# Ring order and modulation chunks in the prologue of a fused two-layer kernel: half of the features first

## The chip, the cores and the metric

The kernel runs on 1 core of one Trainium2 chip. The metric is device microseconds of one execution, as the median of 3 runs. A profile of one execution comes with it.

## The reference, cut to what matters

The reference computes a first block of two layers (gated MLP branch, grouped attention, bidirectional mLSTM), then a second block with dilated attention, a forgetting mixer and expert layers. The change touches only the start of layer 0 of the first block. There, for the latent rows `x` (256 x 1024) and the context rows `ctx` (256 x 1024):

```python
mod_lat = silu(c) @ w_ada[l] + b_ada[l]            # 1024 x 3072: shift, scale, gate, 1024 each
sh, sc, gt = jnp.split(mod_lat, 3, axis=-1)
xn = rms_norm(x, g_norm) * (1 + sc) + sh           # the same for ctx with silu(c_ctx)
...
p = xn @ w_in                                      # 1024 x 3344, in 7 column chunks
```

All of it is in float32. A product of float32 accuracy is made from rounded parts: high x high, high x low, low x high, three matmuls.

## The kernel before

**Ring.** All large weights come through a ring of 6 slots of 1 MB each, in the order of `ring_items()` (L86). An item is half of a chunk (512 of the 1024 rows, 512 columns: 1 MB; the first `w_in` chunk has 272 columns: 0.54 MB). SyncE (SP) walks through the list in order: before it issues item n, it waits until item n-6 is used up (`free(n - RING)`, issue at L322). A first half of a `w_in` chunk is used up once TensorE has done the fourth of the chunk's eight feature blocks (`win_used`), a second half at the chunk's end, an `ada` item once its eight matmuls are done. Between ring items stand, on the same queue, six small loads before item 10 (`EARLY_BEFORE`) and 21 small loads before item 22 (`LATE_BEFORE`, L442): gains, biases, router weights, `w_s`.

The list before: `ada` chunks 0, 1, 2, 3 of layer 0 (items 0 to 7), `w_in` chunk 0 (8, 9), first half of `w_in` chunk 1 (10), `ada` 4 and 5 (11 to 14), second half of `w_in` 1 (15), first half of `w_in` 2 (16), `ada` 0 of layer 1 (17, 18), second half of `w_in` 2 (19), first half of `w_in` 3 (20), `ada` 1 and 2 of layer 1 (21 to 24), second half of `w_in` 3 (25), and so on to item 37.

**Modulation.** A modulation chunk is 512 columns of `w_ada`: `ada_rows` (L2856) multiplies them on TensorE into a PSUM bank (16 matmuls), VectorE copies the bank to SBUF (`ada_copy`, L2271), `ada_row_cols` (L2869) sums and transposes it by 8 small matmuls, VectorE adds the bias (`ada_sums`). Chunks 0 and 1 are the shift of features 0 to 511 and 512 to 1023, chunks 2 and 3 the scale. After all four, VectorE makes `A1 = (1 + scale) * g_norm` and signals `mods_done`.

**Rows.** ScalarE squares and scales the four row tiles (`first_rows`), TensorE transposes them in 8 feature blocks k into PSUM (`norm`, L2823), ScalarE (even k) and VectorE (odd k) apply scale and shift (`transposed_block`, L1995 and L2312), ScalarE rounds to the high part `XH` (L2003), VectorE makes the low part `XL` (L2195).

**Projection.** `project_split` (L2950 to L2952) runs a chunk: for each of the 8 blocks k, four row tiles, three matmuls each. GpSimd (POOL) splits the weights into `WH` (L1852) and `WL` (L1861); the low part of block q comes in its program after the high part of block q+1. Behind chunk k come `ada_row_cols` of what `MODS_BEHIND[0][k-2]` names and `ada_rows` of what `MODS_BEHIND[0][k]` names.

**Hankel.** Six small matmuls on a one-hot table (L3315) make bias rows for the second block. VectorE splits them (L2800), POOL writes them to DRAM and waits for that before it splits any weights.

Of the kernel before, what the change touches and what calls it, by code (L numbers as in the profile page):

```python
# [23 lines left out]
KB = D // 128  # L24
# [59 lines left out]
def ring_items():  # L84
# [52 lines left out]
def build(nc, A, out):  # L137

    es = ExitStack()
    with es:  # L140
# [72 lines left out]
        YP = split("YP", 2 * KB * 256, xt_at).rearrange("p (s k n) -> p s k n", s=2, k=KB)  # L213
        PH = split("PH", 12288, p_at)
        OH = split("OH", 2048, x_at)
        ps = es.enter_context(nc.psum_tensor("ps", [128, 4096], F32))[:, :]
# [47 lines left out]
        for name in ("const_in", "rows_in", "rows_late", "x_in", "oh_in", "chain_dve", "chain_act", "pe_freed", "dve_freed",  # L264
                     "vec_T", "vec_cols", "silu_e", "silu_done", "ada_sums", "ada_cols", "mods_done",
                     "sq_sum", "xs", "xs_T", "xt_act", "xt_dve", "proj", "evict", "a2d", "d2a", "p2d", "d2p",
                     "p2a", "a2p", "row_scores", "row_max", "row_sum", "row_log", "max_rows", "max_T", "shift_rows", "scores", "probs",
# [112 lines left out]

        ADA_ORDER = [(0, ch) for ch in range(4)] + [it[1:] for n in range(7) for it in MODS_BEHIND[0].get(n, ())]

# [4 lines left out]
        def ada_rows_at(a):  # L387

            return bank(3 + a % 3) if a < 4 else bank(4 + a % 3)

# [4 lines left out]
        def ada_cols_at(a):  # L395

            return bank(7 - a % 2 if a < 4 else 7, 8 * a, 8 * a + 8)

# [219 lines left out]
        def pool_block2(pool):  # L618

            def table(part, v, dst, sem_):  # L620
# [5 lines left out]
                pool.dma_start(dst[:, :, 0:cols], src.bitcast(F32R)).then_inc(sem_, 16)  # L626

            pool.wait_ge(S("x_tile"), X_BLOCK1)
            nc.gpsimd.tensor_copy(jrev, K[:, K_J:K_J + 128]).then_inc(S("rounded"), 1)
# [1198 lines left out]
        def _(pool):  # L1828
# [66 lines left out]
        def _(act):  # L1895
# [93 lines left out]

            def transposed_block(k, tiles, scale, shift, dst=None):  # L1990

                act.wait_ge(S("xs_T"), c.up("xs_T", 2) - 1)
                for s in ((0, 1) if len(tiles) == 4 else (0,)):
                    lo, hi = (256, 512) if s == 0 else (0, 256)
                    ins = s_.activation(XT[:, k, lo:hi] if dst is None else dst[:, k, :], bank(k, lo, hi), ACT.Identity,  # L1995
                                        scale=scale(s)[:, k:k + 1], bias=shift(s)[:, k:k + 1])
                ins.then_inc(S("xt_act"), 1)

            def first_layer_rows(scale, shift):

                def high(k):
                    act.wait_ge(S("xt_act" if k % 2 == 0 else "xt_dve"), k // 2 + 1)
                    s_.activation(XH[:, k], XT[:, k], ACT.Copy).then_inc(S("xt_hi"), 1)  # L2003

                first_rows()
                act.wait_ge(S("mods_done"), 1)
                transposed_block(0, range(T), scale, shift)
                transposed_block(2, range(T), scale, shift)
                act.wait_ge(S("hk_out"), 16)
                high(0)  # L2010
                high(1)
                for k in (2, 4, 6):
                    if k + 2 < KB:
                        transposed_block(k + 2, range(T), scale, shift)
                    high(k)
                    high(k + 1)

# [163 lines left out]
        def _(dve):  # L2181
# [99 lines left out]
            def mods(kind, l):  # L2281
# [14 lines left out]
                to("mods_done", ins)  # L2296

            def invert_rstd(tiles):
# [7 lines left out]

            def transposed_block(k, tiles, scale, shift, dst=None):

                dve.wait_ge(S("xs_T"), c.up("xs_T", 2))
                for s in ((0, 1) if len(tiles) == 4 else (0,)):  # L2310
                    lo, hi = (256, 512) if s == 0 else (0, 256)
                    ins = v.tensor_scalar(XT[:, k, lo:hi] if dst is None else dst[:, k, :], bank(k, lo, hi), scale(s)[:, k:k + 1],  # L2312
                                          shift(s)[:, k:k + 1], ALU.mult, ALU.add)
                ins.then_inc(S("xt_dve"), 1)

            def first_layer_rows(scale, shift):
# [9 lines left out]
                for k in (2, 4, 6):  # L2326
                    if k + 2 < KB:
                        transposed_block(k + 3, range(T), scale, shift)
                    low(k)
# [467 lines left out]
            for g in range(3):  # L2797
                dve.wait_ge(S("hk_ps"), g + 1)
                hi, lo = (Qf[0:48, (3 * a + g) * HANKEL:(3 * a + g + 1) * HANKEL] for a in range(2))
                link(v.tensor_copy(hi.bitcast(F32R), bank(g, 0, HANKEL)[0:48, :]))  # L2800
                ins = tt(lo.bitcast(F32R), bank(g, 0, HANKEL)[0:48, :], hi, ALU.subtract)
# [15 lines left out]
        def _(pe):  # L2817
# [54 lines left out]

            def norm(tiles, blocks=range(KB)):
                for k in blocks:
                    for t in tiles:
                        if k == 0:
                            pe.wait_ge(S("xs"), c.up("xs"))
                        ins = tp(bank(k, 128 * t, 128 * t + 128), XS[:, t, 128 * k:128 * k + 128])
                    ins.then_inc(S("xs_T"), 1)
                if k == KB - 1:  # L2880
                    c.up("xt_act", 4)
                    c.up("xt_dve", 4)
                    pe.wait_ge(S("xt_act"), 2)
                    pe.wait_ge(S("xt_dve"), 2)

# [50 lines left out]
            def project_split(n, behind):  # L2936
# [3 lines left out]
                for k in range(KB):  # L2940
# [245 lines left out]
            def block1(l):  # L3186
                L = list(range(T)) if l == 0 else list(LAT)
                n = len(L)
                pe.wait_ge(S("mods_done"), l + 1)
                if l == 0:  # L3190
                    norm(range(T), range(6, KB))
                else:
                    norm_by_tile(range(T), before_last=5, before_chunks=3)
# [115 lines left out]
            ada_rows(0, 0)  # L3309
            ada_rows(0, 1)  # L3310
            pe.wait_ge(S("oh_in"), 16)
            pe.wait_ge(S("rel_in"), 16)
            pe.wait_ge(S("chain_pool"), 1)
            for g in range(3):
                mm(bank(g, 0, HANKEL)[0:48, :], RELB[0:33, :], Pf[0:33, 5000 + g * HANKEL:5000 + (g + 1) * HANKEL],  # L3315
                   start=True, stop=True).then_inc(S("hk_ps"), 1)
# [79 lines left out]
```

## Time and profile before

| | |
|---|---|
| median of 3 runs | 1562.59 us (1561.2 to 1564.77) |
| the profiled execution's own time | 1561.28 us |
| its span | 1559.5 us |
| TensorE busy | 1462.7 us (94%) |
| VectorE, ScalarE, GpSimd busy | 1020.8, 698.0, 224.0 us |
| HBM read | 283.77 MB, mean 183 GB/s |

Times in the trace are microseconds from the span's start. PE is TensorE's matmuls, SPq, POOLq and the like are an engine's queue where it issues DMAs. In a timeline a row is: start, duration, engine, line, operation, output and input, shapes, count; in square brackets the idle time before it and what ended it. Matmuls overlap in their pipeline, so the step between two starts is their cost, not the shown duration.

### The profile page before, as it was taken

The page shows a single profiled execution, that of the slowest core. Times are in us where ns is not written, and L with a number is a line of the kernel's source. Part 1 is how long each engine was busy: PE and PEld are TensorE (multiplying, and loading weights), DVE is VectorE, ACT ScalarE, POOL GpSimd, SP SyncE. Part 2 cuts the span into 40 slices and gives each one's busy share as a digit, 9 for nine tenths or more (in the row PEclk, how much of TensorE's full clock was granted, in tenths as well). Part 3 has the DMA queues.
Part 4 walks back from the last instruction along what each step waited for, and adds up shares of the span by engine and source line. Part 5 has one row for each costly group of instructions (what it writes and reads, how often), then busy time and mean ns, then how long its engine had stood idle before and what let it go on. Part 6 is the DMA issues. An engine that isn't in the chain of part 4 may idle for free.

```text
span 1559.5 us, 19666 instructions
## 1 busy us (share of the span) xinstructions
PE 1462.7 (94%) x7579; PEld 1092.4 (70%) x7579; DVE 1020.8 (65%) x1595; ACT 698.0 (45%) x1129; POOL 224.0 (14%) x240
## 2 busy tenths in 40 slices
PE   5999997989999889999999999899999998889998
PEld 2777772577655454788788877778887876678886
DVE  2418757764475863777677768687775656478776
ACT  3311228323211633655156524556654656356654
POOL 1558721133000201000310020000000004000000
PEclk8999999989999899999999999899998998999999
DMA  9585621202575433677676662398884420098882
GB/s 343 187 264 194 225 68 63 75 28 82 185 247 187 143 116 119 190 245 244 158 226 234 225 183 68 118 324 295 297 275 166 162 93 1 1 314 304 294 302 108
DMA packets 186474, 286.55 MB, mean 184 GB/s; under 512 B 13739, under 2 KB 95115, under 8 KB 186380
## 3 DMA queue, kind: packets, MB, share of 16 engines
q1 hardware_dynamic: 172080, 273.56, 51.4%
q0 software_dynamic: 13200, 8.84, 3.0%
q10 hardware_dynamic: 1100, 2.89, 0.5%
q8 instruction: 60, 0.98, 0.3%
q14 instruction: 34, 0.28, 0.1%
HBM read 283.77 MB, written 1.49 MB: 183 GB/s over the span
## 4 chain that ended last, share of the span: by engine, by line
PE 77%; DVE 13%; ACT 5%; DMA 2%; issue 1%; SPq 1%; POOL 0%; DVEq 0%; ACTq 0%; POOLq 0%
PE ps L1330 40%; PE ps L2932 6%; PE ps L2823 3%; PE ps L2950 3%; PE ps L2952 2%; PE ps L2951 2%; DVE acc L2240 2%; DMA ring<-in_w_ada 2%; ACT ps L2079 2%; DVE P L2195 2%; PE ps L3021 1%; SPq L442 1%; PE ps L2856 1%; PE ps L3004 1%; PE ps L1564 1%
## 5 line engine op out<-in xcount | busy, mean ns | idle before, releaser
L1330 PE MATMUL ps<-WB,YP 128*128 128x512 f32 x1196 | 290.7, 398 | 2.7 <-DVE WB L2195 2.7
L1330 PEld LDWEIGHTS ps<-WB,YP 128*128 128x128 f32 x1196 | 228.7, 193 | 51.5 <-issue 2.2
L2195 DVE TENSOR_TENSOR WP<-ring,WP 128x2048 fp32r<-128x2048 f32 (+1 forms) x102 | 219.2, 2164 | 49.0 <-ACT WP L818 48.8
L1330 PE MATMUL ps<-WP,XP 128*128 128x512 f32 x960 | 231.5, 393 | 6.3 <-DVE WP L2195 6.3
L1330 PEld LDWEIGHTS ps<-WP,XP 128*128 128x128 f32 x960 | 177.6, 188 | 44.5 <-DVE XP L2195 5.0
L818 ACT ACTIVATE WP<-ring 128x2048 fp32r<-128x2048 f32 x94 | 179.5, 1914 | 38.4 <-PE ps L1330 38.4
L2195 DVE TENSOR_TENSOR WB<-ring,WB 128x512 fp32r<-128x512 f32 x192 | 128.1, 690 | 87.5 <-ACT WB L672 85.7
L672 ACT ACTIVATE WB<-ring 128x512 fp32r<-128x512 f32 x192 | 114.1, 628 | 55.0 <-PE ps L1330 55.0
L2932 PE MATMUL ps<-ring,XT 128*128 128x512 f32 (+3 forms) x384 | 132.3, 501 | 1.1 <-ACT XT L2022 1.1
L2240 DVE SCALAR_TENSOR_TENSOR acc<-ring,silu_c,acc 128x512 f32<-128x512 f32 x168 | 127.0, 756 | 4.4
L1330 PE MATMUL ps<-WP,HP 128*128 128x512 f32 x480 | 114.7, 391 | 0.0
L2022 ACT ACTIVATE P<-ps 128x512 f32<-128x512 f32 (+3 forms) x66 | 35.2, 545 | 166.7 <-PE ps L2952 87.5
L2932 PEld LDWEIGHTS ps<-ring,XT 128*128 128x128 f32 x384 | 70.3, 192 | 56.4 <-issue 50.4
L1330 PEld LDWEIGHTS ps<-WP,HP 128*128 128x128 f32 x480 | 90.1, 188 | 19.6 <-issue 1.0
L2950 PE MATMUL ps<-WH,XH 128*128 128x512 f32 (+1 forms) x224 | 86.0, 384 | 2.2 <-DVE XL L2195 1.9
L2951 PE MATMUL ps<-WL,XH 128*128 128x512 f32 (+1 forms) x224 | 84.7, 378 | 0.0
L2952 PE MATMUL ps<-WH,XL 128*128 128x512 f32 (+1 forms) x224 | 84.7, 378 | 0.0
L2453 DVE TENSOR_REDUCE small<-ps 128x2 f32<-128x256 f32 (+3 forms) x68 | 53.5, 786 | 43.8 <-PE ps L1595 18.5
L1861 POOL TENSOR_TENSOR WL<-ring,WH 128x512 fp32r<-128x512 f32 (+1 forms) x56 | 79.9, 1428 | 0.1
L626 POOL DMA_DIRECT2D HBH<-hankel x24 | 16.9, 707 | 283.9 <-PE ps L1631 256.5
L739 ACT ACTIVATE E<-ps 128x512 f32<-128x512 f32 (+1 forms) x24 | 16.1, 670 | 85.6 <-PE ps L1631 43.9
L2950 PEld LDWEIGHTS ps<-WH,XH 128*128 128x128 f32 x224 | 42.8, 191 | 14.4 <-issue 4.2
(420 smaller groups left out, 2279.5 us busy)
## 6 DMA issues: line engine op xcount, KB each, us to landing
ring<-in_w_ada SPq DMA_DIRECT2D x72, 1024.0 KB, 7.5
ring<-in_a_w_in SPq DMA_DIRECT2D x36, 1024.0 KB, 5.2
ring<-in_w_gate SPq DMA_DIRECT2D x64, 512.0 KB, 4.4
ring<-in_w_up SPq DMA_DIRECT2D x64, 512.0 KB, 5.4
ring<-in_w_down SPq DMA_DIRECT2D x32, 1024.0 KB, 6.6
ring<-in_w_in SPq DMA_DIRECT2D x24, 1024.0 KB, 9.6
ring<-in_b_w_in SPq DMA_DIRECT2D x12, 1024.0 KB, 5.0
ring<-in_w_out SPq DMA_DIRECT2D x8, 1024.0 KB, 5.1
```

Source lines behind the costliest of these rows:

```text
L672: s_.activation(block_slot(q)[:, 0], w, ACT.Copy).then_inc(S("b_hi"), 1)
L818: s_.activation(WP[:, (m + 1) % CONV, 0], slot(first + m), ACT.Copy).then_inc(S("w_hi"), 1)
L1330: ins = mm(dst, x(a), w(b), start=(start and n == 0), stop=(stop_ and n == 2))
L1861: nc.gpsimd.tensor_tensor(lo, w, hi.bitcast(F32), ALU.subtract).then_inc(S("win_lo"), 1)
L2195: return v.tensor_tensor(out_, a, b, op)
L2240: ins = v.scalar_tensor_tensor(o, w[:, kk, :], sc, o, ALU.mult, ALU.add)
L2453: ins = v.tensor_reduce(o[n], src, AX.X, ALU.max, negate=True)
L2823: return nc.tensor.transpose(o, i, ident[0:n, 0:n])
L2932: ins = mm(b[:, 0:hi - lo], lhs(half * kk + k, t), w[:, k, lo:hi], start=(half == 0 and k == 0), stop=(half == len(its) - 1 and k == kk - 1))
L2950: mm(b, XH[:, k, cols], hi, start=(k == 0), stop=False)
L2951: mm(b, XH[:, k, cols], lo, start=False, stop=False)
L2952: ins = mm(b, XL[:, k, cols], hi, start=False, stop=(k == KB - 1))
```

## The change

It does six things.

1. The first ten ring items become `ada` 0, `ada` 2, first half of `w_in` 0, `ada` 1, `ada` 3, second half of `w_in` 0.
2. `MODS_BEHIND[0]` goes from two, one, two, one, two chunks behind `w_in` chunks 0 to 4 to one, two, one, two, two. By the rule of the list this gives: 10 `w_in` 1 first half; 11, 12 `ada` 4; 13 `w_in` 1 second half; 14 `w_in` 2 first half; 15, 16 `ada` 5; 17, 18 `ada` 0 of layer 1; 19 `w_in` 2 second half; 20 `w_in` 3 first half; 21, 22 `ada` 1 of layer 1; 23 `w_in` 3 second half; 24 `w_in` 4 first half; 25 to 28 `ada` 2 and 3 of layer 1; 29, 30 second half of `w_in` 4 and first half of 5; 31 to 34 `ada` 4 and 5 of layer 1. From item 31 on both lists are the same. `EARLY_BEFORE` and `LATE_BEFORE` stay 10 and 22.
3. TensorE starts with `ada` 0, the hankel matmuls, `ada` 2 and their columns, transposes feature blocks 0 to 3 and starts `w_in` chunk 0. `ada` 1, `ada` 3, their columns and the transposes of blocks 4 to 7 are put between its blocks 0 to 3.
4. VectorE makes `A1` by halves (`first_mods`, signals `mods_half` and `mods_done`), and scales row tile 2 itself; ScalarE scales the other three.
5. The hankel parts are kept in `P` rather than `Q`; POOL waits for their store only at the start of the second block. ScalarE's sqrt table is loaded before the squares.
6. PSUM homes of the rows, columns and transposed blocks are other banks; `ada_rows` waits from its eighth chunk on until the copy of the chunk three before it is made.

```diff
-MODS_BEHIND = ({0: (('ada', 0, 4), ('ada', 0, 5)), 1: (('ada', 1, 0),), 2: (('ada', 1, 1), ('ada', 1, 2)), 3: (('ada', 1, 3),), 4: (('ada', 1, 4), ('ada', 1, 5))},
+MODS_BEHIND = ({0: (('ada', 0, 4),), 1: (('ada', 0, 5), ('ada', 1, 0)), 2: (('ada', 1, 1),), 3: (('ada', 1, 2), ('ada', 1, 3)), 4: (('ada', 1, 4), ('ada', 1, 5))},
...
+FIRST_MODS = (0, 2, 1, 3)
...
-    for c in range(4):
-        chunk("ada", 0, c * 512, c * 512 + 512)
-    chunk("win", 0, *CHUNKS[0])
+    for half in range(2):
+        for c in FIRST_MODS[2 * half:2 * half + 2]:
+            chunk("ada", 0, c * 512, c * 512 + 512)
+        items.append(("win", 0, *CHUNKS[0], half))
...
@@ GpSimd @@
-                           Qf[0:48, 0:6 * HANKEL].rearrange("c (g j) -> c g j", g=6)).then_inc(S("hk_out"), 16)
-            pool.wait_ge(S("hk_out"), 16)
+                           Pf[0:48, 7000:7000 + 6 * HANKEL].rearrange("c (g j) -> c g j", g=6)).then_inc(S("hk_out"), 16)
...
@@ ScalarE @@
             def first_rows():
 
+                roots_ready()
...
-                for t in range(T):
+                for t in (0, 1, 3):
                     s_.activation(XS[:, t, :], X[:, t, :], ACT.Identity, scale=rstd[:, t:t + 1]
...
                 first_rows()
+                act.wait_ge(S("mods_half"), 1)
+                transposed_block(0, range(T), scale, shift, home=first_home)
+                high(0)
+                transposed_block(2, range(T), scale, shift, home=first_home)
+                high(1)
+                high(2)
+                high(3)
                 act.wait_ge(S("mods_done"), 1)
-                transposed_block(0, range(T), scale, shift)
-                transposed_block(2, range(T), scale, shift)
+                transposed_block(4, range(T), scale, shift, home=first_home)
+                high(4)
+                high(5)
+                transposed_block(6, range(T), scale, shift, home=first_home)
+                high(6)
+                high(7)
                 act.wait_ge(S("hk_out"), 16)
...
@@ VectorE @@
-                transposed_block(1, range(T), scale, shift)
-                transposed_block(3, range(T), scale, shift)
+                transposed_block(1, range(T), scale, shift, home=first_home)
                 low(0)
+                transposed_block(3, range(T), scale, shift, home=first_home)
                 low(1)
...
+                low(2)
+                ada_copy(0, 1)
+                low(3)
+                ada_sums(3, [(0, 1)])
+                ada_copy(0, 3)
+                ada_sums(4, [(0, 3)])
+                to("mods_done", first_mods(4))
...
             invert_rstd(range(T))
-            for ch in range(1, 4):
-                ada_copy(0, ch)
-                ada_sums(ch, [(0, ch - 1)])
-            ada_sums(4, [(0, 3)])
-            mods("ada", 0)
+            to("xs_dve", ts(XS[:, 2, :], X[:, 2, :], rstd[:, 2:3], op0=ALU.mult))
+            ada_sums(1, [(0, 0)])
+            ada_copy(0, 2)
+            ada_sums(2, [(0, 2)])
+            to("mods_half", first_mods(0))
...
@@ TensorE @@
+                if a >= 7:
+                    pe.wait_ge(S("ada_rows_sb"), a - 2)
...
+                    if n == 0:
+                        behind_first_block(k)
...
+            def behind_first_block(k):
+
+                if k == 0:
+                    pe.wait_ge(S("xt_act"), 1)
+                    ada_rows(0, 1)
+                if k == 1:
+                    first_transposes((4, 5))
+                    ada_row_cols([(0, 1)])
+                    pe.wait_ge(S("xt_dve"), 1)
+                    ada_rows(0, 3)
+                if k == 2:
+                    ada_row_cols([(0, 3)])
+                if k == 3:
+                    first_transposes((6, 7))
...
             ada_rows(0, 0)
-            ada_rows(0, 1)
...
             ada_row_cols([(0, 0)])
-            for ch in (2, 3):
-                ada_rows(0, ch)
-                ada_row_cols([(0, ch - 1)])
+            ada_rows(0, 2)
+            ada_row_cols([(0, 2)])
             pe.wait_ge(S("hk_sb"), 1)
-            norm(range(T), range(3))
-            ada_row_cols([(0, 3)])
-            norm(range(T), range(3, 6))
+            first_transposes(range(4))
```

## Rows read from the trace of the kernel before

**Rows 1.** The page: busy time, then the chain that ended last, by engine.

```profile
PE 1462.7 (94%) x7579; PEld 1092.4 (70%) x7579; DVE 1020.8 (65%) x1595; ACT 698.0 (45%) x1129; POOL 224.0 (14%) x240
...
PE 77%; DVE 13%; ACT 5%; DMA 2%; issue 1%; SPq 1%; POOL 0%; DVEq 0%; ACTq 0%; POOLq 0%
```

**Rows 2.** Timeline of TensorE in the prologue.

```profile
13.29 3.64 PE L2856 MATMUL ps<-ring,silu_c 128*32 128x512 f32 x16 [1.78 <-DVE VD L2217]
...
22.46 1.94 PE L2856 MATMUL ps<-ring,silu_c 128*32 128x512 f32 x8 [1.32 <-DMA ring<-in_w_ada]
24.32 4.07 PE L3315 MATMUL ps<-P,RELB 33*48 33x384 f32 x6
...
34.91 1.92 PE L2856 MATMUL ps<-ring,silu_c 128*32 128x512 f32 x16
36.77 1.05 PE L2869 MATMUL ps<-K,acc 128*128 128x2 f32 x8
37.68 1.51 PE L2823 MATMUL ps<-K,P 128*128 128x128 f32 x12
```

**Rows 3.** The chain that ended last, 40 to 62 us: start, length, what.

```profile
40.08 0.18 DVE M L2195
...
40.69 1.07 ACT XT L1995 x3
...
43.17 0.70 DVE XL L2195
...
44.12 0.36 PE ps L2950
...
47.43 3.09 POOL WL L1861
...
58.41 3.57 PE ps L2856 x32
```

**Rows 4.** Timeline of SyncE's queue, 73 to 105 us.

```profile
73.53 1.06 SPq L322 DMA_DIRECT2D ring<-in_w_ada  x2
...
83.99 0.37 SPq L322 DMA_DIRECT2D ring<-in_w_ada  x1
...
86.41 4.39 SPq L442 DMA_DIRECT2D RW<-in_router_expert_w  x1
90.84 2.84 SPq L442 DMA_DIRECT2D WS<-in_w_s  x1
...
102.99 2.17 SPq L322 DMA_DIRECT2D ring<-in_w_ada  x3
```

**Rows 5.** Timeline of TensorE, 85 to 115 us.

```profile
85.20 1.06 PE L2856 MATMUL ps<-ring,silu_c 128*32 128x512 f32 x8 [0.24 <-DMA ring<-in_w_ada]
...
108.09 1.84 PE L2869 MATMUL ps<-K,acc 128*128 128x2 f32 x16
...
113.85 1.06 PE L2856 MATMUL ps<-ring,silu_c 128*32 128x512 f32 x8 [1.21 <-DMA ring<-in_w_ada]
```

**Rows 6.** Stretches: length, busy time (count) by engine, PEclk, DMA share, GB/s.

```profile
45.00:47.00 2.00, 2.00 (x11) 2.00 (x10) 2.00 (x5) 2.00 (x6) 0.00 (x0) 0.50 1.05 389
48.00:50.00 2.00, 2.00 (x19) 2.00 (x18) 1.88 (x4) 0.59 (x2) 2.00 (x1) 1.00 0.63 242
76.00:91.00 15.00, 14.76 (x73) 10.56 (x72) 0.69 (x1) 2.40 (x4) 8.97 (x10) 1.00 1.05 391
```

**Rows 7.** A 1 MB ring item on an idle queue: SyncE's issue, GpSimd's first use.

```profile
126.05 0.37 SPq L322 DMA_DIRECT2D ring<-in_w_in  x1
...
131.15 1.08 POOL L1852 CAST WH<-ring 128x512 fp32r<-128x512 f32 x1 [2.31 <-DMA ring<-in_w_in]
```

**Rows 8.** Timeline of VectorE: after the hankel parts, and at the third chunk.

```profile
29.67 0.18 DVE L2301 RECIPROCAL small<-small 128x4 f32<-128x4 f32 x1
...
29.88 0.69 DVE L2271 COPY acc<-ps 128x512 f32<-128x512 f32 x1
...
142.84 1.42 DVE L2271 COPY acc<-ps 128x512 f32<-128x512 f32 x2
```

More of the change, by code:

```diff
@@ L214, in build @@
         PH = split("PH", 12288, p_at)
+        HK = [[Pf[0:48, 7000 + (3 * a + g) * HANKEL:7000 + (3 * a + g + 1) * HANKEL] for g in range(3)] for a in range(2)]
         OH = split("OH", 2048, x_at)
@@ L265, in build @@
                      "vec_T", "vec_cols", "silu_e", "silu_done", "ada_sums", "ada_cols", "mods_done",
-                     "sq_sum", "xs", "xs_T", "xt_act", "xt_dve", "proj", "evict", "a2d", "d2a", "p2d", "d2p",
+                     "sq_sum", "xs", "xs_T", "xs_dve", "mods_half", "xt_act", "xt_dve", "proj", "evict", "a2d", "d2a", "p2d", "d2p",
                      "p2a", "a2p", "row_scores", "row_max", "row_sum", "row_log", "max_rows", "max_T", "shift_rows", "scores", "probs",
@@ L379, in used @@
             return [(S(name), value) for name, value in (r if isinstance(r, list) else [r])]
-        ADA_ORDER = [(0, ch) for ch in range(4)] + [it[1:] for n in range(7) for it in MODS_BEHIND[0].get(n, ())]
+        ADA_ORDER = [(0, ch) for ch in FIRST_MODS] + [it[1:] for n in range(7) for it in MODS_BEHIND[0].get(n, ())]
         def ada_index(l, ch):
@@ L387, in ada_rows_at @@
         def ada_rows_at(a):
-            return bank(3 + a % 3) if a < 4 else bank(4 + a % 3)
+            return bank((0, 2, 4, 5)[a]) if a < 4 else bank(4 + a % 3)
         def ada_copy_at(a):
@@ L395, in ada_cols_at, with first_home @@
         def ada_cols_at(a):
-            return bank(7 - a % 2 if a < 4 else 7, 8 * a, 8 * a + 8)
+            return bank((1, 3, 4, 5)[a] if a < 4 else 7, 8 * a, 8 * a + 8)
+        def first_home(k):
+            return (4, 5, 6, 7, 6, 7, 4, 5)[k]
         def unit_moe(i, x, t):
@@ L626, in table @@
                 pool.dma_start(dst[:, :, 0:cols], src.bitcast(F32R)).then_inc(sem_, 16)
+            pool.wait_ge(S("hk_out"), 16)
             pool.wait_ge(S("x_tile"), X_BLOCK1)
@@ L1988, in transposed_rows, with transposed_block @@
                     transposed_block(k, tiles, scale, shift, dst)
-            def transposed_block(k, tiles, scale, shift, dst=None):
+            def transposed_block(k, tiles, scale, shift, dst=None, home=lambda k: k):
                 act.wait_ge(S("xs_T"), c.up("xs_T", 2) - 1)
@@ L2005, in first_layer_rows @@
                 first_rows()
-                act.wait_ge(S("mods_done"), 1)
-                transposed_block(0, range(T), scale, shift)
-                transposed_block(2, range(T), scale, shift)
-                act.wait_ge(S("hk_out"), 16)
[L2010 to L2016, printed above, removed]
+                act.wait_ge(S("mods_half"), 1)
[5 more added lines that the diff above has]
+                high(3)
+                act.wait_ge(S("mods_done"), 1)
+                transposed_block(4, range(T), scale, shift, home=first_home)
[4 more added lines that the diff above has]
+                high(7)
+                act.wait_ge(S("hk_out"), 16)
             def evict(dst, src):
@@ L2296, in mods, with first_mods @@
                 to("mods_done", ins)
+            def first_mods(k):
+                for s in range(2):
+                    ins = v.scalar_tensor_tensor(A1[:, 0, s, k:k + 4], M1[:, 0, s, 8 + k:12 + k], 1.0,
+                                                 VA[:, VG + k:VG + k + 4], ALU.add, ALU.mult)
+                return ins
             def invert_rstd(tiles):
@@ L2305, in norm, with transposed_block @@
                     transposed_block(k, tiles, scale, shift, dst)
-            def transposed_block(k, tiles, scale, shift, dst=None):
+            def transposed_block(k, tiles, scale, shift, dst=None, home=lambda k: k):
                 dve.wait_ge(S("xs_T"), c.up("xs_T", 2))
@@ L2320, in low @@
                     tt(XL[:, k], XT[:, k], XH[:, k].bitcast(F32), ALU.subtract).then_inc(S("xt_lo"), 1)
-                transposed_block(1, range(T), scale, shift)
-                transposed_block(3, range(T), scale, shift)
+                transposed_block(1, range(T), scale, shift, home=first_home)
                 low(0)
+                transposed_block(3, range(T), scale, shift, home=first_home)
                 low(1)
-                for k in (2, 4, 6):
-                    if k + 2 < KB:
-                        transposed_block(k + 3, range(T), scale, shift)
+                low(2)
[5 more added lines that the diff above has]
+                to("mods_done", first_mods(4))
+                for k in (4, 6):
+                    transposed_block(k + 1, range(T), scale, shift, home=first_home)
                     low(k)
@@ L2798, in _ @@
                 dve.wait_ge(S("hk_ps"), g + 1)
-                hi, lo = (Qf[0:48, (3 * a + g) * HANKEL:(3 * a + g + 1) * HANKEL] for a in range(2))
-                link(v.tensor_copy(hi.bitcast(F32R), bank(g, 0, HANKEL)[0:48, :]))
-                ins = tt(lo.bitcast(F32R), bank(g, 0, HANKEL)[0:48, :], hi, ALU.subtract)
+                link(v.tensor_copy(HK[0][g].bitcast(F32R), bank(4 + g, 0, HANKEL)[0:48, :]))
+                ins = tt(HK[1][g].bitcast(F32R), bank(4 + g, 0, HANKEL)[0:48, :], HK[0][g], ALU.subtract)
                 if g < 2:
@@ L2871, in ada_row_cols, with first_transposes @@
                 ins.then_inc(S("ada_cols0"), 1)
-            def norm(tiles, blocks=range(KB)):
+            def first_transposes(blocks):
                 for k in blocks:
-                    for t in tiles:
-                        if k == 0:
+                    if k == 4:
+                        pe.wait_ge(S("xt_act"), 2)
+                    if k == 5:
+                        pe.wait_ge(S("xt_dve"), 2)
+                    if k >= 6:
+                        pe.wait_ge(S("ada_sums_done"), k - 3)
+                    for t in (0, 1, 2, 3):
+                        if k == 0 and t == 2:
+                            pe.wait_ge(S("xs_dve"), 1)
+                        elif k == 0:
                             pe.wait_ge(S("xs"), c.up("xs"))
-                        ins = tp(bank(k, 128 * t, 128 * t + 128), XS[:, t, 128 * k:128 * k + 128])
+                        ins = tp(bank(first_home(k), 128 * t, 128 * t + 128), XS[:, t, 128 * k:128 * k + 128])
                     ins.then_inc(S("xs_T"), 1)
[L2880 to L2884, printed above, removed]
             def norm_by_tile(tiles, before_sum=0, before_last=0, before_chunks=0):
@@ L3188, in block1 @@
                 n = len(L)
[L3189 to L3192, printed above, removed]
+                if l == 1:
+                    pe.wait_ge(S("mods_done"), l + 1)
                     norm_by_tile(range(T), before_last=5, before_chunks=3)
@@ L3314, in _ @@
             for g in range(3):
-                mm(bank(g, 0, HANKEL)[0:48, :], RELB[0:33, :], Pf[0:33, 5000 + g * HANKEL:5000 + (g + 1) * HANKEL],
+                mm(bank(4 + g, 0, HANKEL)[0:48, :], RELB[0:33, :], Pf[0:33, 5000 + g * HANKEL:5000 + (g + 1) * HANKEL],
                    start=True, stop=True).then_inc(S("hk_ps"), 1)
             ada_row_cols([(0, 0)])
-            for ch in (2, 3):
-                ada_rows(0, ch)
-                ada_row_cols([(0, ch - 1)])
+            ada_rows(0, 2)
+            ada_row_cols([(0, 2)])
             pe.wait_ge(S("hk_sb"), 1)
-            norm(range(T), range(3))
-            ada_row_cols([(0, 3)])
-            norm(range(T), range(3, 6))
+            first_transposes(range(4))
+            c.up("xt_act", 4)
+            c.up("xt_dve", 4)
             block1(0)
```

4 lines of the change are left out of this document (2 added, 2 removed).

## The prediction, made before the changed kernel was run

> **What bounds the kernel now.** I read the page first: TensorE is busy 94% of the span and holds 77% of the chain that ended last; SyncE's queue and the DMAs hold 3% [rows 1]. TensorE's work is the same before and after, so the change can only move TensorE's waits and its clock. I then read TensorE's timeline of the prologue, where its idle time is. `ada` 1 waits until 22.46 for its second half, the fourth megabyte of the ring; from there TensorE has no gap until the transposes are done, but runs much of it at 1.2 GHz: sixteen `ada` matmuls cost 3.64 there and 1.92 at 34.91 [rows 2]. After the last columns the chain passes through VectorE and ScalarE from 40.08 to 44.12, and only then does `w_in` chunk 0 start [rows 3]. Last I read SyncE's queue, because the change rebuilds the list it walks through. In it the 21 small loads stand between item 21, issued at 83.99, and item 22, issued at 102.99: 18.6 us in which no ring item goes out [rows 4]. TensorE pays little for it: it finishes `w_in` chunk 2 at 108.1 and waits once, 1.21 us, for the last of the items issued behind the small loads [rows 5]. The reader should see that this gap is hidden because item 21 could go out at the end of chunk 1, 24 us before chunk 2's end.
>
> **The prologue, step by step.** `ada` 0 ends at 16.9 as now. The hankel matmuls follow (4.07, half that at 2.4 GHz) and VectorE is done with them 5.35 us after their start (24.32 to 29.67), so by 22.3 [rows 2, 8]. `ada` 2 takes the ring places of `ada` 1, so its last half lands at 22.45 as now. Then: eight matmuls 1.0 (1.94 at the low clock), copy 0.69, columns 1.0 (more at the low clock), sums and `first_mods` 0.6 [rows 2, 3, 8]: `mods_half` at 25.7 to 27.2. From 40.69 to TensorE's start at 44.12 stand 3.4 us, of which the first 1.0 is a second block that ScalarE no longer puts ahead [rows 3]; 2.5 are left. Chunk 0 starts at 28.3 to 29.8; I take 29.3, which is 14.8 earlier than 44.12. But it now carries work: `ada` 1 and 3 (1.9 each), two sets of columns (1.0 each), 16 transposes (about 2) [rows 2]. Block 0 has 12 matmuls, 1.5 at 2.4 GHz, 2.7 at 1.2; I take 2.1: 31.4. `ada` 1's last half lands after 3.1 MB more at 0.39 MB/us and the hankel store, at 30.4 [rows 6], so `ada` 1 is not late; at a mixed clock it ends at 33.9. Block 1, transposes, columns, `ada` 3: 39.3. Block 2, columns, block 3: 43.3. Blocks 4 to 7 and 8 transposes end about 51, where chunk 0 ended at 58.4 before with the work still equal [rows 3]: a gain of 7 us at this point. ScalarE's earlier table load, VectorE's row tile and POOL's removed wait lie beside this and add nothing: POOL's splits need the first `w_in` half, which lands at about 24.
>
> **What the list does to it.** Before, items 10 to 13 could be fetched during the prologue; now item 10 takes the slot of `w_in` 0's first half and waits for block 3, 43.4. Nothing goes out before. `ada` 4's last half (item 12) is third in a row. Before, a third item landed 12.1 us after the first's issue (73.1, just ahead of the 73.53 pair, to 85.2) or 10.8 (102.99 to 113.8) [rows 4, 5]; I take 11.4: 54.8. TensorE is free at 51, so it waits about 3 us and starts chunk 1 at 55.9. A wait of that size can cost the clock: after the 1.9 us idle before 44.12 the granted clock was 0.50 in 45 to 47 and 1.00 again from 48, which is 3.5 us at half speed, 1.75 lost [rows 3, 6]; after 1.21 us idle at 113.85 it was not lost. Chunk 1 takes 21.8 (as chunk 2 from 86.2 to 108.1), with 1.75 of clock ends at 79.5; `ada` 5 and layer 1's `ada` 0 take 3.6 [rows 3, 5]; chunk 2 starts at 83.1, where it started at 86.2 before. The gain is 3 us, with the same work behind it.
>
> Here lies the main term. Item 20 now takes the slot of item 14, first half of `w_in` 2, and so waits for block 3 of chunk 2: 83.1 + 10.9 = 94.0. Items 20 and 21 take 1.0, the 21 small loads 18.6, item 22 goes out at 113.6 and lands 5.1 later, as a single item does [rows 4, 7]: 118.7. TensorE has finished chunk 2 at 104.9, columns at 105.9 and the first half of `ada` 1 at 106.8: it waits 11.9 us. Before, its last wait here ended at 113.85: 4.9 later. Behind that point the changed kernel also has more to do: a whole `ada` chunk (1.9) and one more set of columns (0.9), and after such a wait the clock is low for 3.5 us, 1.75 [rows 5, 6]. Behind chunk 4 five items in a row go out after its block 3, and the fifth is needed 14.7 us later; at 2.7 us each and 5.1 for the first it lands after 15.9: 1 us more. Sum: 4.9 + 1.9 + 0.9 + 1.75 + 1.0 = 10.4 us slower, 8.7 if the first wait does not cost the clock; I take 9.5.
>
> Would the small loads still take 18.6 us? Two rows of 4.39 and 2.84 hold 7.2 of it; the other 19 share 11.4, 0.6 each [rows 4]. Those two look like a full queue: the DMAs ran at 391 GB/s up to 91 [rows 6], just to where the first of the two ends, so 4.6 us or 1.8 MB were still open when it was issued at 86.4. In the changed order items 20 and 21 go out some 2 to 3 us before the same load and leave about 1.5 MB of their 2.1 open, so I take 18.6. If nothing blocked, 21 loads at 0.6 are 12.6: 6.0 less.
>
> The extra wait of `ada_rows` for VectorE's copies costs nothing: VectorE reaches the copies of the third turn at 142.84 [rows 8] after work that the columns behind chunk 2 release, 2 us earlier now, and TensorE asks for the first of them at the end of chunk 4, past 165.
>
> The trace prices the fixed part of a transfer: 5.1 us for 1 MB alone, less 2.7 at 391 GB/s, leaves 2.4. The Trainium skill, page "DMA: Bandwidth & Descriptors", section "Latency and other measured facts", gives about 2 us; by it the landing of item 22, and the sum, would be 0.4 less.
>
> **Rivals.** (a) The small loads go out unblocked in 12.6 us: item 22 lands at 112.7 and the sum is 9.5 - 6.0 = 3.5 slower; with a prologue at the high clock throughout, which gives 2.6 more (28.3 instead of 29.3, and 1.6 in block 0 and `ada` 1), it is 0.9, no measurable change. For it: TensorE's idle time leaves SyncE's queue empty before items 20 and 21; against: the open bytes above. (b) Faster: the pause is covered, so that the 7 us of the prologue are kept. SyncE's shortest issue is 0.37 [rows 4, 7]; 21 of these are 7.8 us, item 22 lands at 107.9, TensorE waits 1.1 at full clock, and the sum is -5.95 + 1.9 + 0.9 + 1.0 = -2.1, or -3.0 if the first wait does not cost the clock: 1559. It decides from small loads of 7.8 us or less; against it stand the 0.6 that they take. (c) POOL's low parts become late in chunk 0. One took 3.09 beside VectorE's two-input operations and held TensorE [rows 3]. Four such are 12.4 where four blocks take 6.0; of the 6.4 the wait for item 12 covers 3: 3.4 more than the main case, 1575. The Trainium skill, page "SBUF — State Buffer", section "Who interferes with whom", says that the two engines hold a shared port pair by an exclusive lock. The 3.09 row fits that, and by the lock the weights of blocks 4 to 7 would be the exposed ones.
>
> **How the numbers follow.** Main case 0.70: 9.5 slower. Rival (a) 0.16, mostly with a better prologue too and then no change; (b) 0.07; (c) 0.07. Against the profiled execution 1561.28 + 9.5 = 1570.8; the median of the runs is 1.3 higher, so 1572.1; I say 1571.5. The range goes down to rival (a) with a good prologue, 1563, and up to (c) with the clock lost twice, 1576; the main case alone is 1567 to 1575. About 0.2%, 3.1 us, is what a measurement tells from no change. Slower by more: 0.70 + 0.07 + 0.03 of (a) = 0.80; within: the other 0.13 of (a); faster: 0.07.
>
> **What would show it.** The profile after should have: chunk 0's first matmul near 29; SyncE issuing nothing from about 33 to 43; a wait of about 3 us for `in_w_ada` before chunk 1; item 21 issued just behind chunk 2's fourth block with 18 us of L442 after it; and a single wait of TensorE of about 12 us before the second half of an `ada` chunk near 107 to 119, with the granted clock at 0.50 behind it. If that last wait is missing or below 5 us, the prediction is wrong in its main term.

## The result, and the profile after

The changed kernel took 1577.2 us (median of 9 runs, 1571.37 to 1595.73), the kernel before 1562.59 beside it (9 runs, 1559.86 to 1571.31): ratio 1.0091, 95% interval 1.0063 to 1.0119, so slower. Predicted were 1571.5 and 1563 to 1576; the sign and the mechanism came as predicted, the median lies 1.2 us above the range. The profiled execution took 1571.92 us against 1561.28 before, 10.6 more; 9.5 was predicted for it. Here and below a median counts all executions, while a ratio and its interval leave out the slow ones, over 1.5% above the fastest of the same kernel, which are one of nine for the changed kernel and four of twelve in the two later runs with medians of 1574.21 and 1571.89 us.

On the page of the changed kernel TensorE has the same work, 0.3 us more busy time, and DMA holds more of the chain that ended last than in [rows 1] (3% against 2%):

```profile
span 1570.1 us, 19676 instructions
...
PE 1463.0 (93%) x7579; PEld 1093.0 (70%) x7579; DVE 1010.4 (64%) x1598; ACT 698.0 (44%) x1129; POOL 212.7 (14%) x240
...
PE 76%; DVE 13%; ACT 5%; DMA 3%; SPq 1%; issue 1%; POOL 0%; DVEq 0%; ACTq 0%
```

TensorE's timeline in the changed kernel, from the prologue (answers to [rows 2, 5]) to the end of layer 0's projections:

```profile
13.20 3.64 PE L2883 MATMUL ps<-ring,silu_c 128*32 128x512 f32 x16 [1.77 <-DVE VD L2230]
16.77 2.46 PE L3360 MATMUL ps<-P,RELB 33*48 33x384 f32 x6
...
22.10 1.94 PE L2883 MATMUL ps<-ring,silu_c 128*32 128x512 f32 x8 [0.69 <-DMA ring<-in_w_ada]
24.92 1.87 PE L2896 MATMUL ps<-K,acc 128*128 128x2 f32 x8 [0.88 <-DVE acc L2284]
26.65 3.65 PE L2848 MATMUL ps<-K,P 128*128 128x128 f32 x16
...
103.47 1.07 PE L2883 MATMUL ps<-ring,silu_c 128*32 128x512 f32 x8
116.58 1.93 PE L2883 MATMUL ps<-ring,silu_c 128*32 128x512 f32 x8 [12.04 <-DMA ring<-in_w_ada]
140.98 1.84 PE L2896 MATMUL ps<-K,acc 128*128 128x2 f32 x16
142.75 3.64 PE L2883 MATMUL ps<-ring,silu_c 128*32 128x512 f32 x32
168.22 0.95 PE L2896 MATMUL ps<-K,acc 128*128 128x2 f32 x8
169.09 1.92 PE L2883 MATMUL ps<-ring,silu_c 128*32 128x512 f32 x16
172.31 1.06 PE L2883 MATMUL ps<-ring,silu_c 128*32 128x512 f32 x8 [1.29 <-DMA ring<-in_w_ada]
174.93 1.94 PE L2883 MATMUL ps<-ring,silu_c 128*32 128x512 f32 x8 [1.55 <-DMA ring<-in_w_ada]
...
228.15 1.07 PE L2848 MATMUL ps<-K,P 128*128 128x128 f32 x8
```

and two rows of the kernel before, for the stage behind chunk 4 and for the end of the projections:

```profile
163.40 3.64 PE L2856 MATMUL ps<-ring,silu_c 128*32 128x512 f32 x32
...
217.42 1.07 PE L2823 MATMUL ps<-K,P 128*128 128x128 f32 x8
```

The reader should see one wait of 12.04 us between the two halves of layer 1's `ada` 1, and eight matmuls behind it that cost 1.93 instead of 1.07. SyncE's queue in the changed kernel says why (it answers to [rows 4]):

```profile
92.32 0.51 SPq L326 DMA_DIRECT2D ring<-in_w_ada  x1
92.87 0.50 SPq L450 DMA_DIRECT2D GH<-in_g_head  x1
...
95.06 2.14 SPq L450 DMA_DIRECT2D RW<-in_router_expert_w  x1
97.25 3.54 SPq L450 DMA_DIRECT2D WS<-in_w_s  x1
...
110.89 0.44 SPq L326 DMA_DIRECT2D ring<-in_w_ada  x1
```

Item 21 goes out at 92.32, then the 21 small loads, and item 22 only at 110.89: 18.0 us. The stretches of the changed kernel (columns as in [rows 6]) show the cost in clock:

```profile
84.00:106.00 22.00, 20.54 (x99) 16.41 (x97) 2.25 (x3) 3.67 (x5) 14.59 (x16) 1.00 0.49 129
106.00:117.00 11.00, 0.42 (x4) 0.20 (x8) 10.02 (x16) 0.33 (x1) 0.00 (x0) 0.51 0.53 165
117.00:121.00 4.00, 4.00 (x16) 2.11 (x9) 3.76 (x8) 0.00 (x0) 0.00 (x0) 0.64 1.05 392
121.00:143.00 22.00, 22.00 (x109) 18.43 (x111) 9.99 (x13) 3.60 (x5) 15.91 (x16) 1.00 0.57 196
```

The granted clock was full (2.4 GHz) up to the wait, half (1.2 GHz) in it and for some 3 us behind it. The group of matmuls at 228.15 stood at 217.42 before: 10.7 us. From there to the last matmul the two traces stay 10.5 to 10.7 us apart, so the profiled difference lies wholly ahead of 228 us.

### The profile page after: what moved, and what is told of

The parts are those of the page before. It is cut to its first block, busy times and chain, and to the rows that moved or that the text cites. A ratio compares the mean times of both kernels' runs of the same rounds, so it can differ in the third digit from the quotient of the medians.

```text
span 1570.1 us, 19676 instructions
## 1 busy us (share of the span) xinstructions
PE 1463.0 (93%) x7579; PEld 1093.0 (70%) x7579; DVE 1010.4 (64%) x1598; ACT 698.0 (44%) x1129; POOL 212.7 (14%) x240
## 4 chain that ended last, share of the span: by engine, by line
PE 76%; DVE 13%; ACT 5%; DMA 3%; SPq 1%; issue 1%; POOL 0%; DVEq 0%; ACTq 0%
PE ps L1339 40%; PE ps L2963 6%; DMA ring<-in_w_ada 3%; PE ps L2848 3%; PE ps L2981 3%; PE ps L2982 2%; PE ps L2983 2%; DVE acc L2253 2%; ACT ps L2092 2%; DVE P L2208 2%; PE ps L2883 1%; PE ps L3069 1%; SPq L450 1%; PE ps L3052 1%; PE ps L1573 1%
## 5 line engine op out<-in xcount | busy, mean ns | idle before, releaser
L1869 POOL TENSOR_TENSOR WL<-ring,WH 128x512 fp32r<-128x512 f32 (+1 forms) x56 | 70.4, 1259 | 0.1
```

Source lines behind the costliest of these rows:

```text
L1869: nc.gpsimd.tensor_tensor(lo, w, hi.bitcast(F32), ALU.subtract).then_inc(S("win_lo"), 1)
```

## The experiments

Each run was timed beside executions of the kernel before. "Lead" is how far a kernel's profiled execution is ahead of (-) or behind (+) the kernel before's at one matmul of the attention (at 295.1 us in the kernel before), and then at the last matmul.

**The changed kernel again.**

> The changed kernel once more, unaltered, to see how its runs spread beside runs of the kernel before on one chip. The profiled execution was 10.6 us over that of before, the median of nine runs 14.6 over. If the spread belongs to single executions (TensorE's clock), I expect 1571 to 1580 in most and the profile again near 1572; if something in the kernel is different from run to run, the profile should show a wait that the first did not have.

Measured: 1577.63 us (6 runs), ratio 1.0106 (1.0065 to 1.0147). Lead +11.2 and +13.4. The result stands. This profiled execution took 1574.65 us, 2.7 more than the first of the same kernel (1572 was expected), and 2.1 of it arose far behind the changed stage: between 578 and 595 us the granted clock was low here and full there. Stretch 575 to 600 us in the first, then in this one:

```profile
575.00:600.00 25.00, 20.60 (x141) 14.15 (x142) 18.93 (x49) 5.55 (x9) 0.00 (x0) 1.00 0.07 22
...
575.00:600.00 25.00, 23.05 (x123) 18.92 (x124) 15.06 (x43) 5.55 (x9) 0.00 (x0) 0.66 0.07 22
```

**The small loads elsewhere, in the changed kernel.**

```diff
-EARLY_BEFORE, LATE_BEFORE = 10, 22
+EARLY_BEFORE, LATE_BEFORE = 10, 20
```

> The changed kernel with LATE_BEFORE 20 instead of 22: the 21 small loads go out after item 19, at the end of chunk 1 (77 us), while SyncE would wait for block 3 of chunk 2 anyway. Theory (the small loads between items 21 and 22 are the cost): the 12.04 us wait before the second half of layer 1's ada 1 goes, with 1.7 us of low clock behind it; the profiled execution is 13 to 14 us shorter than that of the changed kernel, 1558 to 1559, so 2 to 3 below before. Rival (the new order of the ring itself costs): item 20 is now up to 3 us late, TensorE waits for another item in the same place and at most half of the 12 us comes back, 1565 or more.

Measured: 1568.01 us (12 runs), ratio 1.0013 (0.9984 to 1.0042). Lead -2.0, then +7.8. TensorE in this kernel:

```profile
106.00 1.92 PE L2883 MATMUL ps<-ring,silu_c 128*32 128x512 f32 x16
...
161.95 1.06 PE L2883 MATMUL ps<-ring,silu_c 128*32 128x512 f32 x8 [1.65 <-DVE acc L2284]
163.57 1.07 PE L2883 MATMUL ps<-ring,silu_c 128*32 128x512 f32 x8 [0.55 <-DMA ring<-in_w_ada]
...
215.42 1.07 PE L2848 MATMUL ps<-K,P 128*128 128x128 f32 x8
```

All sixteen matmuls of `ada` 1 run in one piece: the 12 us wait is gone, and the last row, 228.15 in the changed kernel and 217.42 before, stands at 215.42. So the wait came from the small loads' place. The expected 1558 to 1559 for the profiled execution was missed (1569.08): the lead of -2.0 is as expected, but +7.8 stands at the end. That arose later, which the clock runs below take up.

The same edit with 15 instead of 20:

> The changed kernel with LATE_BEFORE 15: the 21 small loads go out behind item 14, from about 48 us, before ada 5's first half, where SyncE waits for chunk 0's end and then for block 3 of chunk 1. Items 15 and 16 go out at 66 to 67 as SyncE had to wait for block 3 of chunk 1 until then anyway. By the small-loads theory the 12 us wait is gone as with 20, and here no item 20 is late either: block 1 ends 2 to 3 us earlier than before's. Rival: ada 5's first half and ada 0 of layer 1 come late behind chunk 1, a wait of 1 to 3 us there.

Measured: 1575.48 us (12 runs), ratio 1.0034 (0.9998 to 1.0069). Lead +7.7, then +17.3. The 12 us wait is gone here too, but the loads now hold up the items needed behind chunk 1, as the rival said. Five ring items stand just ahead of them, and they took 22.3 us (50.42 to 72.76), so item 15 went out at 72.76 and not at 66 to 67:

```profile
82.29 1.06 PE L2883 MATMUL ps<-ring,silu_c 128*32 128x512 f32 x8 [1.51 <-DMA ring<-in_w_ada]
85.00 1.06 PE L2883 MATMUL ps<-ring,silu_c 128*32 128x512 f32 x8 [1.65 <-DMA ring<-in_w_ada]
87.71 1.94 PE L2883 MATMUL ps<-ring,silu_c 128*32 128x512 f32 x8 [1.65 <-DMA ring<-in_w_ada]
```

**The same move in the kernel before** (`LATE_BEFORE` 20).

> The kernel before with the 21 small loads ahead of item 20 instead of item 22, nothing else. Theory (the small loads cost only where the order of the list puts them behind a late item): the old list hid them, so block 1 can end at most 1.2 us earlier (the one wait for item 25's group) and at most 1.5 us later; profiled block 1 end within 1.5 us of 217.4, apart from the prologue's clock. Rival (the small loads' place is worth something in any list, so that the changed prologue has no gain of its own): block 1 ends 2 us or more earlier than before's, as in the changed kernel with the same place.

Measured: 1567.6 us (12 runs), ratio 1.0006 (0.9976 to 1.0036). Lead +2.8, then +12.4. The old list gains nothing. At the end of chunk 0, ahead of the small loads, this execution stood at -2.8 by scatter alone. Behind chunk 2 TensorE then waited 0.83 and 1.65 us for `ada` items where the kernel before waited 1.21, and at 197 us 2.63 us for VectorE where it waited 0.51; from there the lead was +1.5. The rival of a gain of 2 us or more falls: from its new place on this execution lost some 4 us, 1.3 of them in the waits behind chunk 2; why VectorE was late is open. The end's +12.4 has a later cause, the long clock drop shown below.

**The change without its list** (the old `MODS_BEHIND`, the new prologue).

```diff
-MODS_BEHIND = ({0: (('ada', 0, 4),), 1: (('ada', 0, 5), ('ada', 1, 0)), 2: (('ada', 1, 1),), 3: (('ada', 1, 2), ('ada', 1, 3)), 4: ...
+MODS_BEHIND = ({0: (('ada', 0, 4), ('ada', 0, 5)), 1: (('ada', 1, 0),), 2: (('ada', 1, 1), ('ada', 1, 2)), 3: (('ada', 1, 3),), 4: ...
```

> The changed prologue with the old list MODS_BEHIND (two, one, two, one, two). Theory: the small loads are hidden as before, but items 10 to 14 all wait for block 3 of chunk 0 and go out in a row at 43.6; the fifth lands at about 61, so chunk 1 starts at 62 as before and the whole gain of the prologue is lost in one wait of 6 us before ada 5's second half, with its clock: 1561 to 1564. Rival (the prologue's 6.5 us gain stays, only the new order of the later chunks costs): 1556.

Measured: 1574.21 us (12 runs), ratio 1.0042 (1.0011 to 1.0074). Lead +6.0 and +6.0. TensorE in this kernel:

```profile
59.49 1.94 PE L2883 MATMUL ps<-ring,silu_c 128*32 128x512 f32 x8 [3.17 <-DMA ring<-in_w_ada]
62.21 1.94 PE L2883 MATMUL ps<-ring,silu_c 128*32 128x512 f32 x8 [0.78 <-DMA ring<-in_w_ada]
...
117.30 1.07 PE L2883 MATMUL ps<-ring,silu_c 128*32 128x512 f32 x8 [1.38 <-DMA ring<-in_w_ada]
```

The 12 us wait needs the new list; the new prologue with the old one waits right behind chunk 0 instead, for transfers that could not go out before block 3, and is slower too: its profiled execution took 1567.21 us where 1561 to 1564 were expected. The reason for a new list is real, and neither list as it stands pays.

**Keeping TensorE busy through the wait.**

```diff
+                    if (l, ch, half) == (1, 1, 0):
+                        pe.wait_ge(S("ada_rows_sb"), 7)
+                        keep_warm(12, 6)
```

> The changed kernel with 12 warming matmuls between the halves of layer 1's ada 1. The first try with 46 was mispriced: a float32 matmul of 512 columns took 0.86 us there, not 0.23, so it filled 40 us. Twelve fill 10.3 of the 12.0 us wait. Theory: the landing does not move, the clock stays at 2.4 GHz behind the wait, 1.7 us shorter: profile at 1568 to 1571. The median tells whether the clock's state at this wait widens the spread: 1574 or less if so, 1576 if not.

Measured: 1572.89 us (12 runs), ratio 1.0079 (1.0044 to 1.0114). Lead +11.3, then +11.0.

```profile
106.37 10.57 PE L2860 MATMUL ps<-K 128*128 128x512 f32 x24
118.80 1.07 PE L2883 MATMUL ps<-ring,silu_c 128*32 128x512 f32 x8 [1.86 <-DMA ring<-in_w_ada]
```

The eight matmuls behind the wait ran at the high clock (1.07), but the clock was not kept: behind the 1.86 us that were left of the wait it fell all the same, 1.5 us after TensorE went on, and stood at 0.57 in the mean of 120 to 124 us. The item came 2.2 us later than in the changed kernel, as all ahead of it was 1.9 later. The profiled time, 1572.27 us, gained nothing; 1568 to 1571 were expected. The median is below the 1574 that was to tell whether the clock's state at this wait widens the spread, but the ratio's interval overlaps those of the changed kernel and the runs still spread from 1566.83 to 1595.09, so it doesn't tell. A first try had 46 such matmuls: each took 0.86 us, 39.8 in all, and filled far more than the pause.

> The changed kernel with 46 matmuls of 512 columns on constants, into a free PSUM bank, put between the two halves of layer 1's ada 1, where TensorE waited 12.04 us; the rest is unaltered. Theory: the wait's landing time does not move, only the clock stays at 2.4 GHz behind it, worth 1.7 us. If the wide spread of the changed kernel's runs comes from how long the clock stays low after this wait, the median falls by more, toward the profiled execution, and the spread narrows. Rival: nothing but 1.7 us or less, and the spread stays.

Measured: 1604.25 us (6 runs), ratio 1.025 (1.0203 to 1.0297). It tells nothing of the wait.

**Delays alone.** The first runs left a puzzle: medians stood further from the kernel before's than the profiled stages. One idea was that what the later stages lose depends on where their waits fall against the moments at which the clock changes; the expectations call it the grid, later Theory A. To try it, extra matmuls on constants were put ahead of layer 0's attention, in the kernel before (1, 2, and 3 with a shorter fourth) and in the changed one (3, so that it should stand 10.6 + 3.0 = 13.6 us behind the kernel before). The expectations count them as 1.0 us each; the traces show 0.86 each, so 0.9, 1.7, 2.9 and 2.6 us in all. Theory A forecast medians of 1566 and 1576 for the last two. The edit, for one:

```diff
                     pe.wait_ge(S("evict"), c.at("proj"))
-                    keep_warm(1, 0)
+                    keep_warm(2, 0)
```

> The kernel BEFORE with one more warming matmul (1.0 us) just ahead of layer 0's attention; it has no other effect on any wait. Background: the changed kernel's profiled execution is 10.6 over before, its median 14 to 15 over, and in one of its variants the whole difference stood in one stretch (305 to 343 us) in which the granted clock was 0.50 where it is 1.00 in before. [...] Then 1.0 us of delay gives a median more than 1 us above before, with a wider spread. Rival (the changed code itself makes the tail slower): exactly 1.0 more, with the spread of before.

> The kernel BEFORE with two more warming matmuls (2.0 us) at the same place. Theory of the grid: a median that is not simply 2.0 above before, and another spread than with 1.0 us; together with the 1.0 us kernel the two medians do not lie on a line. Rival: 2.0 more, spread of before.

> The kernel before with 3.4 us of extra matmuls on constants ahead of the attention of layer 0 (one and two such matmuls, 1.0 and 2.0 us, cost the median 9 us). [...] Theory B (any delay there costs the later stages their clock, whatever its length): 1572 to 1576. Theory C (the extra matmuls at full rate just ahead of the attention themselves bring the drop): 1575 or more, growing with their number.

> [...] Theory A (place against the clock's changes): the later stages run as before's, median 1562.6 + 13.6 = 1576, no later than without the extra matmuls (1577.4). Theory B (a plain delay): 1577.4 + 3.0 = 1580.4.

Measured, with the median of the kernel before beside it where that is not 1562.6 or 1562.7:

| kernel | median us (12 runs) | ratio, 95% interval | lead, attention and end |
|---|---|---|---|
| before, 0.9 us more | 1572.11 | 1.0049 (1.0018 to 1.0080) | -0.7, +5.5 |
| before, 1.7 us more | 1571.84 | 1.0052 (1.0017 to 1.0086) | +2.6, +8.4 |
| before, 2.9 us more | 1565.59 (before 1563.5) | 1.0026 (0.9999 to 1.0053) | +4.2, +14.0 |
| changed, 2.6 us more | 1576.18 (before 1564.6) | 1.0071 (1.0038 to 1.0105) | +12.4, +12.5 |

The 0.9 us of delay cost the median 9 (7.7 by the ratio), the 2.6 us in the changed kernel cost it none (1577.2 and 1577.6 without). A plain delay explains neither. What makes such a jump possible is how the kernel before's own times lie. Of its 122 executions beside these runs, 78 took 1556.9 to 1568.5 us, 40 took 1569.4 to 1578.4, 4 took over 1584, and the medians of the two groups, 1561.6 and 1571.9, are 10 us apart. A median moves by up to that when the larger group changes: of the 12 executions with 0.9 us more, 8 took over 1570. That the upper group are the executions with the drop shown next, which costs 10 us, fits but is not shown, as no execution of that group was profiled. Ahead of the edit, where the three delayed copies are the kernel before word for word, their executions stood at -2.1, -0.2 and +2.2 us against it (at 209.7 us in before): so much does the prologue scatter by itself. The changed kernel's three executions stood at +10.7, +11.3 and +11.6 there. What it hits is seen in one row of stretches, 293 to 331 us, of the kernel before:

```profile
293.00:331.00 38.00, 31.43 (x240) 26.40 (x239) 31.08 (x81) 10.98 (x18) 4.19 (x5) 0.87 0.00 1
```

and of the same kernel with 0.9 us more:

```profile
293.00:331.00 38.00, 36.84 (x197) 31.00 (x198) 22.46 (x63) 6.06 (x9) 3.49 (x4) 0.54 0.00 0
```

Both have the same 1.63 us wait of TensorE for VectorE just ahead (1.64 in the second). In the one the granted clock stays at 1.00 until about 314 and is low for 10 us, in the other it falls at 296, within 2 us of the wait's end, and is low for 37.5 us, and 43 fewer matmuls get done. That stretch took the lead from -0.7 to +9.4. The page's clock line of the kernel before, 40 slices of 39 us, shows it as a 9 and an 8 in the eighth and ninth slice:

```profile
PEclk8999999989999899999999999899998998999999
```

and that of the changed kernel with `LATE_BEFORE` 20 shows 7s in both, the same drop, which took its lead from -2.0 to +8.2:

```profile
PEclk9999999779999999999999999899998998999999
```

Four of the 17 profiled executions had it (this one, the kernel before with 0.9 and with 2.9 us more, and the kernel before with `LATE_BEFORE` 20, whose lead it took from +2.8 to +13.1). The 2.9 us case had it in its profile (+14.0) and yet a median of only +2, so an execution's luck varies too.

**Placing the better list against the clock.** The changed kernel with `LATE_BEFORE` 20, and two, one and minus one of those matmuls (`keep_warm(3, 0)`, `keep_warm(2, 0)`, and none).

> The changed kernel with the small loads ahead of item 20, and 2.0 us of extra matmuls ahead of the attention, so that from there on it stands where the kernel before stands (it was 2.0 us ahead). Theory A (place against the clock's changes): median within 2 us of the kernel before, 1562 to 1565, lower than without the extra matmuls (1568.0). Theory B (a plain delay): 1570 or more.

> The same kernel as in the run that gave 1559.8 us and a ratio of 0.995 to the kernel before, again. If that is a property of the kernel: median 1558 to 1562, ratio 0.993 to 0.998. If it was chance: 1564 to 1570, ratio 1.00 or more.

> The changed kernel with the small loads ahead of item 20 and 1.0 us of extra matmuls: 1.0 us ahead of the kernel before from the attention on. Theory A with a narrow favourable place: between 1561.6 and 1568, near the 1568.0 without extra matmuls. If the favourable place is wide, or the extra matmuls themselves help (theory C): 1559 to 1562.

> The changed kernel with the small loads ahead of item 20, and without the one matmul on constants ahead of the attention of layer 0, so that from there on it is up to 1.0 us further ahead (3.0 of before). [...] Theory B (plain): 1568.0 - 1.0 = 1567. If that matmul was what kept the clock up there: 1570 or more with a low clock just behind it.

| `LATE_BEFORE` 20 and | median us (12 runs), kernel before's | ratio, 95% interval | lead, attention and end |
|---|---|---|---|
| two more | 1559.76, 1563.5 | 0.9950 (0.9924 to 0.9975) | -1.0, -1.7 |
| two more, again | 1564.29, 1564.6 | 0.9998 (0.9958 to 1.0038) | +1.6, +3.9 |
| one more | 1571.89, 1564.6 | 0.9978 (0.9937 to 1.0019) | -1.0, +11.1 |
| one less | 1561.87, 1563.5 | 0.9996 (0.9969 to 1.0022) | +0.4, -0.4 |

The 0.5% of the first run did not come again, so no version is shown to beat the kernel before; with the small loads ahead of item 20 the change is even with it. The same kernel's two medians lie 4.5 us apart, of which 1.1 is also in the kernel before's beside them. At the point of 209.7 us, ahead of the extra matmuls, the five executions with `LATE_BEFORE` 20 stood at -2.0, -3.1, -2.2, -2.8 and -0.6: the new prologue keeps some 2 us there, which the prologue's own scatter and the later clock hide.

## Where the prediction was right, and which step failed

**Right: the prologue.** Chunk 0 started at 30.36 (29.3 predicted) and ended at 51.9 (51), the wait behind it was for item 12 as said, 1.16 us instead of 3, and cost no clock: chunk 1 started at 55.15 (55.9). Chunk 2 started at 80.70 instead of 83.1, block 3's end let SyncE go on at 91.9 instead of 94.0.

**Right: the main term.** 21 small loads in 18.0 us (18.6), the wait 12.04 (11.9), its end at 116.58 (118.7). As everything ahead of it was 2 us earlier, it ended 2.7 later than [rows 5]'s 113.85 instead of 4.9. Behind it the low clock cost 1.5 (1.93 for 1.07, and 0.65 on the next three matmuls; 1.75 predicted), the `ada` chunk 1.8 and the columns 0.9, as said. The run with `LATE_BEFORE` 20 shows that the small loads' place is the cause, and the kernel before, with them ahead of the same item and a wait of 1.21 us, that it costs only with the new list. Rival (a) is refuted, since its bound of 12.6 us for the loads was reached in no trace: the shortest was 15.1 us, ahead of item 20 (79.44 to 94.56). Rival (b) needed 7.8. One sum of (a) was off by its own terms: the prologue at the high clock gives 1.0 + 0.6 + 0.6 = 2.2 and not 2.6, which leaves 1.3 slower instead of 0.9 and changes no chance.

**Mis-sized: behind chunk 4.** 1.0 was allowed; two waits of 1.29 and 1.55 came, and the clock fell behind them (1.94 for eight matmuls), some 4 us in all. The sum by the measured terms: 2.7 + 1.5 + 1.8 + 0.9 + 4 = 10.9, against 10.7 in the trace. So 2.2 too much in one term and 3 too little in another nearly cancelled: that 9.5 came so near to 10.6 is in part luck.

**Rival (c)** did not come: the matmuls of chunk 0 waited 0.93 once for VectorE's low part and never for GpSimd, whose eight low parts took 0.75 to 0.77 us each where rival (c) had 3.09.

**Failed: "the median of the runs is 1.3 higher, so 1572.1".** The step from the profiled execution to the median was taken over from the kernel before as a constant. In the changed kernel it is 5.3 (1577.2 against 1571.92), and the range's upper end, 1576, was built from rivals alone, with nothing for it. The runs show how large that term can be: one kernel's medians of 12 runs were 4.5 us apart, and 0.9 us of delay moved one by 9. The second profiled execution of the changed kernel shows where part of it arises: it was 2.7 us longer than the first, 2.1 of it behind 500 us, with the low clock from 578. The ratio's interval, 1.0063 to 1.0119, is 1572.4 to 1581.2 us and holds 1562.6 + 10.6 = 1573.2. So the 10.6 us of the profile are explained step by step, and the other 4 us need no second mechanism of the change. That they come from clock drops in later stages is shown for single executions, and for the median only made likely by the delays and by the kernel before's two groups of times.

**Open.** What makes an execution meet the long drop is not known. Theory A, that the place against the clock's changes decides, gave right medians for the two delays that were sized by it (1565.59 and 1576.18). But these delays were really 2.9 and 2.6 us, one of them had the long drop in its profile, and the version with two more did not repeat: it is not shown.

## What to carry to other kernels

When a list of transfers is reordered, look at what else stands on the same queue at a fixed place in it. A block of small loads, 18 us of issue here, was nearly free while the items ahead of it went out early, and most of its length (12 us) became a wait once they had to wait for the consumer. Move such a block with the list, and price it in the list that it will stand in, for two places in the new list (ahead of item 20 and of item 15) differed by 10 us at the attention. And carry the runs' scatter into the range: look at all times of the kernel before, and if they lie in two groups, here 10 us apart, a small change can move the median by most of that gap, and the step from one profiled execution to the median is not a constant.

## What the runs showed of the hardware

The same wait of 1.63 us ahead of the same work was followed by 10 us of low clock in one execution and by 37.5 us in another, with TensorE busy 31.43 and 36.84 of the 38 us from 293 on: once low in the second, the clock stayed low although TensorE was hardly idle. A wait of 1.16 us with nothing added (behind chunk 0) cost no clock, one of 1.55 (behind chunk 4, after another of 1.29) did. Twelve matmuls on constants in the 12 us wait held the granted clock at 1.00 up to the item's arrival at 118.80, but it fell at 120.3, behind the 1.86 us of wait that were left. And the same 21 small loads took longer the more ring items had gone out just ahead of them on the queue: 15.1 to 15.4 us with one (five traces of the changed kernel with `LATE_BEFORE` 20), 18.0 to 18.6 with two (five traces with 22), 22.2 with four (the kernel before with `LATE_BEFORE` 20, 72.65 to 94.81) and 22.3 with five (`LATE_BEFORE` 15).
